# Out-projection of the recurrent mixer: its sums and the turn of its rows moved into the block of the recurrence

## What is computed

```python
def rwkv7_scan(r, w, k, v, kk, a):
    def step(state, inp):
        r_t, w_t, k_t, v_t, kk_t, a_t = inp
        sa = jnp.einsum('bhvk,bhk->bhv', state, -kk_t)
        state = (state * w_t[:, :, None, :] + sa[..., None] * (kk_t * a_t)[:, :, None, :]
                 + v_t[..., None] * k_t[:, :, None, :])
        return state, jnp.einsum('bhvk,bhk->bhv', state, r_t)
...
def rwkv7_mixer(...):
    ...
    for d in range(2):                       # forwards and backwards
        ...
        o = rwkv7_scan(*ins)
        bonus = jnp.sum(rh * kd * r_k.astype(F32), axis=-1, keepdims=True) * vh
        dir_out.append((group_norm(o, gn_w, gn_b) + bonus.reshape(nB, S, D)) * g.astype(F32))
    y = dir_out[0] + dir_out[1]
    return y.astype(h.dtype) @ w_o
```

## Time and profile before

| | us |
|---|---|
| three runs: median (lowest to highest) | 2849.84 (2845.86 to 2853.01) |
| the profiled execution: time | 2848.72 |
| its span in the trace | 2847.0 |
| mean granted TensorE clock in it, of full speed | 0.962 |
| TensorE matmul rows busy | 2661.1, 93% |
| VectorE, ScalarE, GpSimd busy | 673.1, 429.7, 88.1 |

### The profile page before, as it was taken

The page is one execution under the profiler, slowest core; times in us unless marked ns, Lnnn a source line. Parts: engine busy times, 40 slices in busy tenths (PEclk is TensorE's granted clock), DMA queues, the critical chain, the costliest instruction groups (busy, mean ns, idle before and its releaser), DMA issues. The chain is left out here.

```text
span 2847.0 us, 76137 instructions
## 1 busy us (share of the span) xinstructions
PE 2661.1 (93%) x34649; PEld 2210.2 (78%) x34649; DVE 673.1 (24%) x1724; ACT 429.7 (15%) x1039; POOL 88.1 (3%) x168
## 2 busy tenths in 40 slices
PE   8899999989989999999999999899989799989998
PEld 7677777668769999989989988666658588876664
DVE  5411000271120110110110110410043567761001
ACT  1111000110110110110110110400011344441000
POOL 0100000010000000000000000000000000010000
PEclk9899999989989999999999999999999888889999
DMA  7344444534429999999999994364452000002442
GB/s 220 114 133 134 133 148 133 160 125 133 148 96 399 407 407 407 408 407 407 408 407 407 407 376 129 111 201 156 145 164 74 5 5 6 6 4 97 152 158 88
DMA packets 290525, 571.23 MB, mean 201 GB/s; under 512 B 18326, under 2 KB 181140, under 8 KB 290404
## 3 DMA queue, kind: packets, MB, share of 16 engines
q1 hardware_dynamic: 290404, 569.49, 55.3%
HBM read 568.37 MB, written 5.28 MB: 201 GB/s over the span
## 5 line engine op out<-in xcount | busy, mean ns | idle before, releaser
L1738 PE MATMUL ps<-xg,ring 128*64 128x80 f32 x14336 | 518.2, 234 | 7.9 <-issue 2.7
L1738 PEld LDWEIGHTS ps<-xg,ring 128*64 128x64 f32 x14336 | 505.6, 138 | 18.8 <-DMA ring<-in_moe_w_up_dram 8.9
L1333 PE MATMUL ps<-xT,ring 128*128 128x256 f32 x1728 | 381.5, 380 | 4.6 <-PEq L452 3.0
L1333 PEld LDWEIGHTS ps<-xT,ring 128*128 128x128 f32 x1728 | 329.2, 191 | 66.4 <-issue 22.4
L1345 PE MATMUL ps<-ring,hidden 128*128 128x512 f32 x688 | 301.8, 592 | 0.0
L1754 PE MATMUL ps<-hidden,expert_down 128*64 128x80 f32 x7168 | 259.7, 233 | 9.3 <-DVE hidden L1830 5.2
L1754 PEld LDWEIGHTS ps<-hidden,expert_down 128*64 128x64 f32 x7168 | 251.9, 137 | 15.2 <-DVE hidden L1830 6.9
L1345 PEld LDWEIGHTS ps<-ring,hidden 128*128 128x128 f32 x688 | 130.7, 190 | 147.5 <-issue 145.4
L618 PE MATMUL ps<-ring,xT 128*128 128x256 f32 (+1 forms) x1056 | 226.4, 377 | 7.0 <-PEq L1214 3.7
L618 PEld LDWEIGHTS ps<-ring,xT 128*128 128x128 f32 x1056 | 197.0, 194 | 35.1 <-issue 8.8
L618 PE MATMUL ps<-xT,ring 128*128 128x256 f32 (+1 forms) x944 | 213.9, 388 | 10.2 <-PEq L596 4.5
(11 more groups left out here) (380 smaller groups left out, 2505.4 us busy)
## 6 DMA issues: line engine op xcount, KB each, us to landing
ring<-in_moe_w_gate_dram SPq DMA_DIRECT2D x128, 896.0 KB, 16.6
ring<-in_moe_w_up_dram SPq DMA_DIRECT2D x128, 896.0 KB, 16.7
expert_down<-in_moe_w_down_dram SPq DMA_DIRECT2D x96, 1024.0 KB, 17.3
ring<-in_mlp_w_dram SPq DMA_DIRECT2D x64, 1024.0 KB, 5.4
ring<-in_w_xkv_dram SPq DMA_DIRECT2D x16, 1024.0 KB, 5.3
expert_down<-in_moe_w_down_dram SPq DMA_DIRECT2D x32, 512.0 KB, 16.5
ring<-in_ffn_w_gate_dram SPq DMA_DIRECT2D x11, 1024.0 KB, 5.4
ring<-in_ffn_w_up_dram SPq DMA_DIRECT2D x11, 1024.0 KB, 5.3
```

Of the source, the lines that this page charges most:

```text
L1333: mm = pe.matmul(bank[:, m * SEQ:(m + 1) * SEQ], w[:, c, m * P:(m + 1) * P], self.xT[:, c, :], start=(c == 0), stop=(c == KC - 1))
L1738: mm = pe.matmul(bank[b][o:o + HEAD, at, :], w[:, c, f * P + o:f * P + o + HEAD], xg[:, p * E_STEP + c, :], start=(p == 0 and c == 0 and a ...
```

## The change

`turn_only` and `add_rows` are no longer called here; their work is in the block of `chunks`. In the last pair TensorE turns the rows of the seven finished column blocks between the steps of the solve, 14 transposes in groups of four, four, four and two, into the banks of A and B. VectorE copies them to xT ahead of the last output. Behind the last pair TensorE adds the first six sums over these seven blocks into the banks A, B and G (42 matmuls), turns the last block once the last output is written, adds the seventh sum over seven blocks, then the last block to these seven sums, and then the whole eighth sum. VectorE and ScalarE copy the sums out as before. The four loads of the next MLP are issued as soon as the factors were made for the last time.

```diff
@@ -2289,7 +2289,7 @@
             s.over(n)
-    def chunks(self, ctx, y):
+    def chunks(self, ctx, y, into, loads):
@@ -2380,6 +2380,27 @@
         def chunk(s, d):
             return d if s == 0 else 1 - d
+
+
+        LAST = pairs - 1
+        turned_banks = (A(0), B(0), A(1), B(1))
+        sums = [(n // TT, n % TT) for n in range(8)]
+        sum_banks = (A(0), B(0), A(1), B(1), G(0), G(1), C(1), C(0))
+        FIRST_SUMS = 6
+        run, xT = m.run, m.xT
+        first_piece = run.taken
+        VECTOR_TURNS = len(turned_banks) + 1
+
+        def turned_at(c):
+
+            if c == LAST:
+                return ps[:, C(0), 0:SEQ]
+            return ps[:, turned_banks[c // 2], (c % 2) * SEQ:(c % 2 + 1) * SEQ]
+
+        def sum_into(n):
+            p, t = sums[n]
+            return into[:, t, p * 256:(p + 1) * 256]
+
         with m.block() as block:
             @block.sync
             def _(sp):
@@ -2390,6 +2411,9 @@
                         wait(sp, "gates_done", i - 1, 2)
                     for d in range(2):
                         sp.dma_start(g2[:, d, :], g2_src[:, d, columns(i)]).then_inc(q["slice_loaded"].sem, 16)
+
+                wait(sp, "made_ready", LAST, 2)
+                loads(sp)
             @block.gpsimd
             def _(pool):
@@ -2519,6 +2543,11 @@
                             wait(act, "output_over", i - 1, d + 1)
                         act.activation(o[d][:], ps[:, C(d), 0:2 * P], ACT.Copy).then_inc(q["out_ready"].sem, 1)
+                def take_sums():
+                    for n in range(1, 8, 2):
+                        act.wait_ge(m.product_done.sem, m.product_done.at(n + 1))
+                        act.activation(sum_into(n), ps[:, sum_banks[n], 0:256], ACT.Copy).then_inc(m.evac_act.sem, 1)
+
                 begin(0)
                 for d in range(2):
                     exps_first(0, d)
@@ -2529,6 +2558,7 @@
                     pair(i, i == 0, i == pairs - 1)
                 for d in range(2):
                     normalise(pairs - 1, d)
+                take_sums()
             @block.tensor
             def _(pe):
@@ -2672,6 +2702,37 @@
                         mm = by_halves(pe, ps[:, C(d), at:at + HEAD], GM[d][:, 2 * t + hh, 1, :], sa[d][:, t, hh, :], start=False, stop=(s == 1 and hh == 1))
                     if s:
                         mm.then_inc(q["out_done"].sem, 1)
+
+                def turn(c):
+                    wait(pe, "output_over", c, 2)
+                    for t in range(TT):
+                        mm = pe.transpose(turned_at(c)[:, t * P:(t + 1) * P], y[:, t, columns(c)], m.ident[:])
+                    mm.then_inc(m.turned.sem, 1)
+
+                def add_to(n, c):
+                    p, t = sums[n]
+                    w = run.place(first_piece + p)
+                    mm = pe.matmul(ps[:, sum_banks[n], 0:256], xT[:, c, t * P:(t + 1) * P], w[:, c, :], start=(c == 0), stop=(c == KC - 1))
+                    if c == KC - 1:
+                        mm.then_inc(m.product_done.sem, 1)
+
+                def project_out():
+                    for p in range(4):
+                        pe.wait_ge(m.piece_loaded[(run.first + first_piece + p) % RING], run.value[first_piece + p])
+                    pe.wait_ge(m.evac_dve.sem, m.evac_dve.at(len(turned_banks)))
+                    wait(pe, "second_ready", LAST, 4)
+                    for c in range(LAST):
+                        for n in range(FIRST_SUMS):
+                            add_to(n, c)
+                    wait(pe, "out_ready", LAST, 2)
+                    turn(LAST)
+                    for c in range(LAST):
+                        add_to(FIRST_SUMS, c)
+                    pe.wait_ge(m.evac_dve.sem, m.evac_dve.at(VECTOR_TURNS))
+                    for n in range(FIRST_SUMS + 1):
+                        add_to(n, LAST)
+                    for c in range(KC):
+                        add_to(FIRST_SUMS + 1, c)
                 def pair(i, last):
                     for k in range(1, LEVELS):
@@ -2691,10 +2752,19 @@
                             steps(i, k, d)
                     for d in range(2):
                         solve_first(i, 0, d)
+                    if last:
+                        turn(0)
+                        turn(1)
                     for d in range(2):
                         carry(i, 0, d)
+                    if last:
+                        turn(2)
+                        turn(3)
                     for d in range(2):
                         solve_second(i, 0, d)
+                    if last:
+                        turn(4)
+                        turn(5)
                     for d in range(2):
                         state(i, d)
                     for d in range(2):
@@ -2703,6 +2773,8 @@
                         right_sides(i, 1, d)
                     for d in range(2):
                         solve_first(i, 1, d)
+                    if last:
+                        turn(6)
                     for d in range(2):
                         carry(i, 1, d)
                     if not last:
@@ -2723,6 +2795,7 @@
                     gram(0, d)
                 for i in range(pairs):
                     pair(i, i == pairs - 1)
+                project_out()
             @block.vector
             def _(dve):
@@ -2908,8 +2981,22 @@
                     front(0, d)
                 for i in range(pairs):
                     pair(i, i == 0, i == pairs - 1)
-                for _ in output(pairs - 1):
+                for b, bank in enumerate(turned_banks):
+                    n = min(2, LAST - 2 * b)
+                    dve.wait_ge(m.turned.sem, m.turned.at(2 * b + n))
+                    dve.tensor_copy(xT[:, 2 * b:2 * b + n, :].rearrange("p c s -> p (c s)"), ps[:, bank, 0:n * SEQ]).then_inc(m.evac_dve.sem, 1)
+                for _ in output(LAST):
                     pass
+                dve.wait_ge(m.turned.sem, m.turned.at(pairs))
+                dve.tensor_copy(xT[:, LAST, :], turned_at(LAST)).then_inc(m.evac_dve.sem, 1)
+                for n in range(0, 8, 2):
+                    dve.wait_ge(m.product_done.sem, m.product_done.at(n + 1))
+                    dve.tensor_copy(sum_into(n), ps[:, sum_banks[n], 0:256]).then_inc(m.evac_dve.sem, 1)
+        run.taken += 4
+        m.turned.over(pairs)
+        m.product_done.over(8)
+        m.evac_dve.over(VECTOR_TURNS + 4)
+        m.evac_act.over(4)
 def network(nc, I, out):
@@ -2963,9 +3050,7 @@
                     mixer.project()
                 plan = m.second_plan(1, 7)
                 with ExitStack() as work:
-                    mixer.chunks(work, u)
-                m.turn_only(u, m.xT, loads=lambda sp: plan.begin(sp, plan.kinds))
-            m.add_rows(m.xT, 256, u, add=False)
+                    mixer.chunks(work, u, u, lambda sp: plan.begin(sp, plan.kinds))
             m.close_and_norm(u, True, "norm2_12", m.xT)
             m.next_gain = gains[1, 3:4, :]
             m.ffn(plan, None, 0, u, False)
```

## The result

The changed kernel takes 2831.01 us (median of five runs, 2826.27 to 2834.6) where the kernel before takes 2849.84 (five runs, 2845.86 to 2853.01): a ratio of 0.9934, 95% interval 0.9921 to 0.9947, 18.8 us less. The forecast was 2835.2, 14.1 us less by its sum, with 2830.5 to 2842.5 as the range: 2831.01 lies 0.5 us inside its lower end. The profiled execution took 2828.31 us, with a span of 2826.6 and a mean granted clock of 0.969 (before: 2847.0 and 0.962).

What follows compares the result with a forecast made beforehand. TensorE, busy 93% of the span, was taken as the bound. Terms -15.0 + 0.23 + 0.6 + 0.1 = -14.1 us gave 2834.6 from the profiled execution and 2835.8 from the median; forecast 2835.2, range 2830.5 to 2842.5.

Steps and rivals of the forecast that it cites:

- The hole: TensorE's idle time between recurrence and out-projection, 15.0 us, goes; two transposes for the last block add 0.23 us.
- the six waits: TensorE's waits between recurrence and sums, all on things long done: 0 to 0.3 us, taken as 0.1.
- The cover: VectorE's 2.5 us of copies to xT fit its idle time; the last output has 8.9 us to spare beside the sums.
- The transposes: 14 transposes within the last pair's solve, partly taken up by small gaps: +0.6 us, bounds up to 3.0 us above.
- rival C: Fuller work keeps the clock up in the last pair: 15.9 us less, 2833.9 us, chance 0.11.
- The clock behind the hole: Full clock assumed at the start of the sums, since no hole follows: 0, bounds 0 and +1.7 us.
- The loads: Four 1 MB loads of the next MLP, issued earlier beside pairs 6 and 7: no gain and no cost, 0.
- Rival E: Early loads disturb the pair, its instruction stream waiting behind 4 MB: at most 10.8 us back, 2846.5 us, chance 0.05.
- rival A: The forecast as summed, early sums filling the hole: 2835.2 us, own range 2832 to 2838, chance 0.62.
- B: Transposes lie on the last pair's path and the sums start at half clock: 9.8 us less, 2840.0 us, chance 0.13.
- D: Early sums are held up until the last output is over; 5.6 us less 0.8 saved, 2845 us, chance 0.04.
- F: The out-projection's sums run at half clock: up to 13.3 us slower, 2863.1 us, chance 0.05.

Runs made afterwards that it cites:

- sums_late: Changed kernel plus one TensorE wait for the end of the last output before the first sum; 2845.97 us, ratio 0.9995 to the kernel before.
- only_loads_early: Kernel before with only the four loads of the next MLP issued early, when factors were last made; 2845.23 us against 2848.08, ratio 0.9989.
- output_longer: Changed kernel with 32 extra VectorE copies between its copies to xT and the last output; 2836.52 us in one execution.
- turns_behind: Changed kernel with all 14 transposes behind the last pair's solve instead of within it; 2832.3 us, ratio 0.9949 to the kernel before.
- loads_late: Changed kernel with the four MLP loads issued when the last output is over, as before; 2831.52 us, ratio 0.9944 to the kernel before.
- turns_spread: Changed kernel with late MLP loads and the 14 transposes in seven places of two; 2831.18 us, ratio 0.9947 to the kernel before.
- after: The changed kernel's profiled execution, no further edit; 2828.31 us, where the median of its five runs is 2831.01 us.

## Why the prediction was right, and where its terms were off

**The hole.** Forecast -15.0 + 0.23 + 0.1 = -14.7 from the last L136 row to the next block; measured 28.80 - 43.64 = -14.84. sums_late parts it: the wait put back 9.5 us of hole and with it 2.8 us of half clock, and without these two its c would be 38.4 us, 5.2 less than before for the turn and the border that no longer stand ahead of the sums. The 0.1 for the six waits was too much: the first row of the sums starts 0.07 us ahead of the modelled end of the last L136 row. Of the 1.1 us that I gave to a block's end and start, 0.8 were SyncE's issue of the fourth load (only_loads_early); it made no difference to the sum, since both went.

**The cover.** VectorE's copies in its idle time and 8.9 us of room for the output: both as forecast (2.2 and 8.8 us), and output_longer used 8.3 us of the room at no cost.

**The transposes.** +0.6 forecast, 10.03 - 9.47 = +0.56 measured, but right by luck. Their own cost is 1.40 us (turns_behind). I had assumed that the gaps take most of them; they took 14 x 0.117 + 4 x 0.12 - 1.40 = 0.7 us. The other part, 0.85 us, is the half-clock stretch of before that no other kernel of the study has in its last pair. That was rival C's effect; I had put it in the bounds and not in the sum, and the transposes' price was too low by as much.

The rule on transposes that I weighed (the Trainium skill, "TensorE: Matmul & The Clock Gate", Part 4: PE-mode transpose: they don't count as busy for the clock) would have kept the stretch at half, or made it longer. The trace differs: with 14 transposes and nothing else new ahead of them (loads_late) the granted clock is 1.00 over b, where the kernel before has 0.82. The measurement decides: here they did no harm to the clock. That they kept it up is not shown apart from their moving the rows behind them in time, since the early loads alone ended the stretch too.

**The clock behind the hole.** This is the term that was missing. I set the clock's share at the start of the sums at 0, "no hole follows", and took the out-projection and the MLP as equally long in both kernels. In the profiled execution of before the sums were at full clock, so the row looked free; the slow stretch stood 42 us behind their start, in the MLP (2611.0). Over all executions c + d is 293.3 to 293.6 before and 276.8 after, 16.5 to 16.9 us less where the sum had 14.7. That stretch was in the trace that I forecast from. It goes with the hole in this sense: of six executions with a hole five have a slow stretch behind it (1.7 us in the four of before, 2.8 us in sums_late), of eight without none. only_loads_early, with a hole and no such stretch, shows that a hole doesn't always bring one, and what decides it is not shown.

**The loads.** Forecast 0. They cost 0.3 to 0.4 us in the last pair with the rest of the change in place (loads_late, a); and on the kernel before they gave 2.9 us (only_loads_early): 0.6 of them because the block of the turn no longer waits for SyncE, the rest a change of the clock's stretches, whose cause is argued from one trace. Rival E's stall of up to 10.8 us didn't come, but a pause of 0.3 us did. The prediction names rows that stand still during the loads as a sign of being wrong, and by that sign the 0 was wrong, by this little.

**The total.** a to d: 312.4 after, 328.0 to 328.3 before, 15.6 to 15.9 us less whichever two one takes. By terms, with the 1.7 us of the slow stretch: -14.84 + 0.56 + 0.4 - 1.7 = -15.6, where the sum had -14.1. The medians gave 18.8 and 16.7 us; their 95% intervals, 15.1 to 22.5 and 11.4 to 19.1 us, both hold the traces' 15.7, so no further gain is shown. What the medians have beyond it, 1 to 3 us, put 2831.01 below rival A's own range, 2832 to 2838. It lies in the part that both kernels share, in the profiled pair visibly in the first three pairs of the recurrence: 50.6 + 36.9 + 37.2 = 124.7 us against 53.6 + 37.65 + 37.6 = 128.9. Whether it is chance is not settled: a first pair of under 51 us was seen in four of nine executions of changed kernels and in none of five with the order of before, which chance alone gives about once in eight such samples, and nothing of the change is executed ahead of it.

**The rivals.** A was right in its mechanism. B's turns did lie on the path, but at full clock: 1.40 us where it had 3.0 at half, and its slow start of the sums didn't come. C was nearest to the size, 15.9 forecast and 15.7 found, and that is luck: it had b shorter by 1.1 us, and b grew by 0.56; the 1.7 us came from behind the hole, which C doesn't touch. D is what sums_late does: 4.8 us less than before forecast, 3.2 found from a to d. F, the sums at half clock, happened among the changed kernels in sums_late only, for 5.8 us, and then recovered. The other rule I weighed (the Trainium skill, "TensorE: Matmul & The Clock Gate", "A second HAM failure mode: psum-queue depth-cycling") has nothing for it here: six banks in turn or one at a time, 18.40 us and a clock of 1.00.

turns_spread and loads_late are 0.3 to 0.4 us shorter than `after` from a to d, both by the late loads; their times can't be told from the changed kernel's.

## What to carry to other kernels

A hole in the bounding engine costs its length and can also cost slow rows behind it, and those may stand tens of us later and in another block, so compare the whole rest of the program over several executions, not the touched stretch in one. Work that fills such a hole is worth most when it is ready ahead of time: here 42 of 64 matmuls needed only what was finished, and one wait put back in front of them took 12.5 of the 15.7 us. See also which stream ends a block last: here it was for 0.8 us the one that only issues loads. Gaps between dependent steps don't make small pieces of other work free there; group them, and measure them against the same stretch at the same clock.

## What the runs showed of the hardware that I had not expected

- Behind an idle stretch of 9.5 us TensorE ran at half clock for 5.8 us of unbroken work (sums_late), where the transposes of the earlier trace rows had it back after 3.2 us.
- Two unlike small changes, 14 transposes in the solve or four transfers moved ahead of it, each went with the end of a half-clock stretch that stood in all four executions of the kernel before (0.82 against 1.00 over the 9 to 10 us of b).
- The sixth and the seventh pair of the recurrence took 37.53 to 37.55 us in every execution, whatever the first ones took (first pair 50.1 to 53.6 us), and in all fourteen traces the clock falls to half 10.4 us ahead of ScalarE's copy of the seventh pair's outputs. So the end of the recurrence meets the clock in the same way each time: b is 9.46 to 9.47 in four executions of before and 10.02 to 10.05 in all with transposes in the solve.
- A group of transposes between 64x64 rows costs about 0.12 us besides its 0.117 us a row.
- Of the four 1 MB loads that SyncE issues in a row, the first three issues took 0.4 to 0.6 us each and the fourth 3.2 to 3.6 us, in all fourteen executions; in the kernel before a block's end waited for it.
- With the loads early TensorE paused once in dense 64x64 rows, for 0.2 to 0.4 us, about when the last load landed (9.6 to 9.9 us behind the copy, the pause at 9.7): in eight executions of eight, and in none of six with late loads.
